# Opening of a two-layer hybrid encoder kernel: first input weights in four parts behind the modulation quarters, token factor applied to x early, one more slab and the offsets summed on TensorE, two low parts made on GpSimd

## The reference

```
c_act = silu(c)
mod   = c_act @ w_ada[0] + b_ada[0]        # (1, 3072): shift, scale, gate
h     = rms(x) * norm_w * (1 + scale) + shift
proj  = h @ w_in[0]                        # q, k, v are its first 768 columns
```

## Time and profile before

| | before |
|---|---|
| median of 3 runs | 1134.92 us |
| the profiled execution | 1134.01 us |
| its span, first to last instruction | 1132.3 us |
| TensorE busy | 1112.1 us, 98% of the span |
| DVE, ACT, POOL busy | 58%, 47%, 50% |
| mean granted TensorE clock | 0.994 |

### The profile page before, as it was taken

How to read it: one execution, slowest core, us unless ns; L and a number is a source line. 1 busy time by engine, 2 the same in 40 slices (tenths; PEclk the granted TensorE clock), 3 DMA queues, 4 the chain that set the end, 5 groups by cost and what they waited for, 6 DMA issues and landing times.

```text
span 1132.3 us, 15212 instructions
## 1 busy us (share of the span) xinstructions
PE 1112.1 (98%) x5807; PEld 917.6 (81%) x5807; DVE 660.6 (58%) x830; ACT 532.6 (47%) x930; POOL 561.7 (50%) x412
## 2 busy tenths in 40 slices
PE   6999999999999999999999999999999999999997
PEld 5778888888888888888898788888788887888885
DVE  4716465668788545538870635664887854131365
ACT  5544266655545533224462535666546553232234
POOL 5535444535445546545914363445355535464455
PEclk8999999999999999999999999999999999999999
DMA  9656423234443456653304463224433523443332
GB/s 322 208 134 197 132 76 93 76 112 131 129 119 84 129 177 199 206 156 104 96 20 101 142 205 93 76 75 120 130 99 99 132 73 87 116 133 94 105 100 93
DMA packets 203481, 140.79 MB, mean 124 GB/s; under 512 B 12001, under 2 KB 191249, under 8 KB 203409
## 3 DMA queue, kind: packets, MB, share of 16 engines
q1 hardware_dynamic: 202632, 138.91, 42.5%
q10 hardware_dynamic: 776, 0.91, 0.3%
HBM read 136.64 MB, written 2.63 MB: 123 GB/s over the span
## 4 chain that ended last, share of the span: by engine, by line
PE 95%; DVE 2%; SPq 1%; DMA 1%; issue 0%; POOL 0%; ACT 0%; DVEq 0%; POOLq 0%
PE main L683 77%; PE psC L683 6%; PE psA L683 5%; PE psB L683 4%; SPq L398 1%; DMA big<-in_w_ada 1%; PE psB L916 1%; PE psB L896 1%; DVE h_lo L1552 1%; SPq L426 0%; DVE psC L1505 0%; DVE tmp L1547 0%; PE psC L925 0%; POOL tmp L627 0%; DVE tmp L1505 0%
## 5 line engine op out<-in xcount | busy, mean ns | idle before, releaser
L601 POOL TENSOR_TENSOR w_lo<-raw,w_hi 128x512 fp32r<-128x512 f32 x344 | 502.3, 1481 | 537.4 <-ACT w_hi L1101 537.2
L683 PE MATMUL main<-h_hi,w_hi 128*128 128x512 f32 x976 | 388.7, 399 | 3.1 <-ACT h_hi L1101 2.9
L683 PE MATMUL main<-h_hi,w_lo 128*128 128x512 f32 x976 | 379.5, 390 | 0.0
L683 PE MATMUL main<-h_lo,w_hi 128*128 128x512 f32 x976 | 379.3, 390 | 0.0
L1101 ACT ACTIVATE w_hi<-raw 128x512 fp32r<-128x512 f32 x344 | 199.9, 623 | 286.1 <-PE main L683 161.8
L683 PEld LDWEIGHTS main<-h_hi,w_hi 128*128 128x128 f32 x976 | 183.6, 188 | 49.4 <-issue 11.1
L683 PEld LDWEIGHTS main<-h_hi,w_lo 128*128 128x128 f32 x976 | 183.2, 188 | 38.9
L683 PEld LDWEIGHTS main<-h_lo,w_hi 128*128 128x128 f32 x976 | 183.3, 188 | 38.0 <-issue 1.9
L1874 DVE TENSOR_TENSOR tmp<-main,misc 128x512 f32<-128x512 f32 x32 | 22.1, 692 | 165.3 <-PE main L683 162.8
L1713 DVE SCALAR_TENSOR_TENSOR misc<-main,cols,misc 128x511 f32<-128x511 f32 (+2 forms) x96 | 71.9, 749 | 60.9 <-ACT misc L1101 58.3
L683 PE MATMUL main<-y_hi,w_hi 128*128 128x512 f32 x256 | 100.5, 393 | 0.0
(11 more groups left out here) (288 smaller groups left out, 1411.8 us busy)
## 6 DMA issues: line engine op xcount, KB each, us to landing
raw<-in_w_in SPq DMA_DIRECT2D x124, 512.0 KB, 3.9
xbc<-in_w_ada SPq DMA_DIRECT2D x16, 512.0 KB, 4.9
zs<-in_w_ada SPq DMA_DIRECT2D x16, 512.0 KB, 4.6
raw<-in_w_pc SPq DMA_DIRECT2D x16, 512.0 KB, 3.8
raw<-in_w_out SPq DMA_DIRECT2D x16, 512.0 KB, 3.6
zs<-in_w_ada SPq DMA_DIRECT2D x16, 256.0 KB, 7.6
xbc<-in_w_in SPq DMA_DIRECT2D x8, 512.0 KB, 7.6
big<-in_w_ada SPq DMA_DIRECT2D x16, 256.0 KB, 7.2
```

The source lines that it names most:

```text
L601: nc.gpsimd.tensor_tensor(lo_b[:, cut, :], raw_b[:, cut, :], hi_b[:, cut, :].bitcast(F32), ALU.subtract).then_inc(s_split[b], 2 * BT_ // kt)
L683: return nc.tensor.matmul(o, a, b_, start=start, stop=stop)
```

## The change

1. **Weights in four parts.** `wide(part)` loads two k of all six tiles by two DMAs (256 KB and 512 KB, the latter with 512 columns in a row instead of 256) behind each quarter: q0, part 0, q1, part 1, q2, part 2, q3, part 3. ACT rounds a part by three instructions (two tiles each, `wide_hi_part`), POOL subtracts by three (`split_wide`). The number of elements of an instruction stays 512 a partition, and the number of instructions 12 in all.
2. **x takes the token factor early.** DVE multiplies xT by 1/rms in place (`x_scale`) for blocks 0 to 3: block 0 before the first modulation, 1 to 3 behind it. For these blocks ACT makes `h_hi` straight from xT with scale and shift (`h_high_first`), and no longer waits for h_32; DVE makes h_tmp with the shift in it from SBUF alone (`h_32_first`, a tensor_scalar). Blocks 4 to 7 keep the old way.
3. **TensorE sums one slab more** in quarter 0 (slab 4), behind the matmuls that spread 1/rms; DVE has five.
4. **TensorE adds the offsets** b_ada in each quarter by one matmul with the identity; `quarter_mod` has two small DVE operations instead of three.
5. **GpSimd makes the low parts of blocks 0 and 1**; DVE makes those of 2 to 7.
6. Orders: ACT does its quarter 2 products half before and half behind the high parts of blocks 2 and 3, and a part of the weights behind each quarter's products; POOL does part q of the weights, then the sums of quarter q+1.

```diff
-BY_PE = (2, 3)
+BY_PE = (2, 3, 4)
@@ SP
-            quarter(0)
-            wide(0)
-            quarter(1)
-            quarter(2)
-            wide(1)
-            quarter(3)
+            for q in range(QUARTERS):
+                quarter(q)
+                wide(q)
@@ POOL
+            def split_wide(part):
+                cut = slice(2 * part, 2 * part + 2)
+                for u in range(U_GA):
+                    pool.wait_ge(s_hiw, couple_count(u, 2 * part))
+                    nc.gpsimd.tensor_tensor(couple_lo[u][:, :, cut, :],
...
-                    for u, b in WIDE[:5]:
-                        split_half(l, u, b, 0)
-                    add_products(1)
-                    split_half(l, 2, 1, 0)
-                    add_products(2)
-                    for u, b in WIDE:
-                        split_half(l, u, b, 1)
-                    add_products(3)
+                    for q in range(QUARTERS):
+                        split_wide(q)
+                        if q < QUARTERS - 1:
+                            add_products(q + 1)
+                        if q == 0:
+                            for k in range(2):
+                                pool.wait_ge(s_h32, k + 1)
+                                pool.wait_ge(s_hhi, k + 1)
+                                nc.gpsimd.tensor_tensor(h_lo[:, k], h_tmp[k], h_hi[:, k].bitcast(F32), ALU.subtract
+                                                        ).then_inc(s_h, 1)
@@ PE, quarter_sums
+                pe.wait_ge(s_cols, 1)
+                mm(quarter_ps[q], ident[:, :],
+                   cols[:, 0, V_BADA:V_BADA + 2 * KT].rearrange("p (w k) -> p w k", w=2)[:, :, 2 * q:2 * q + 2], False, True
+                   ).then_inc(s_adam, 1)
...
             first_rows()
             spread(psC0, rms, 1)
+            slab_sums(BY_PE[2:])
             quarter_sums(0)
@@ ACT
+            def h_high_first(k):
+                act.wait_ge(s_mod, k // 2 + 1)
+                act.wait_ge(s_xs, k + 1)
+                f(h_hi[:, k, :], xT[:, k, :], ACT.Identity, scale=mod[:, 0, KT + k:KT + k + 1], bias=mod[:, 0, k:k + 1]
+                  ).then_inc(s_hhi, 1)
@@ DVE
             def quarter_mod(q):
+                k0, k1 = 2 * q, 2 * q + 2
                 dve.wait_ge(s_adam, q + 1)
-                modulation(0, quarter_ps[q], 2 * q, 2 * q + 2)
+                stt(mod[:, 0, KT + k0:KT + k1], quarter_ps[q][:, 2:4], 1.0, cols[:, 0, V_NORM + k0:V_NORM + k1], ALU.add,
+                    ALU.mult)
+                nc.vector.tensor_copy(mod[:, 0, k0:k1], quarter_ps[q][:, 0:2]).then_inc(s_mod, 1)
+                dve.wait_ge(s_mod, q + 1)
+            def x_scale(k):
+                tt(xT[:, k], xT[:, k], psC0, ALU.mult).then_inc(s_xs, 1)
+            def h_32_first(k):
+                dve.wait_ge(s_xs, k + 1)
+                ts_(h_tmp[k], xT[:, k], mod[:, 0, KT + k:KT + k + 1], mod[:, 0, k:k + 1], ALU.mult, ALU.add
+                    ).then_inc(s_h32, 1)
...
```

More of the change, by code:

```diff
@@ L209, in build @@
         s_raw, s_split = sem2("raw_loaded"), sem2("w_split")
-        s_rawx = [[sem(f"raw_wide_loaded{u}{half}") for half in range(2)] for u in range(3)]
+        s_xs, s_mod = sem("x_scaled_in_opening"), sem("modulation_done")
+        s_rawx = [sem(f"raw_wide_loaded{part}") for part in range(QUARTERS)]
         s_hi = sem2("w_hi_done")
@@ L408, in load @@
                 if (l, u) == (0, U_GA):
-                    for e in range(2):
-                        sp.wait_ge(s_split[e], part_count(0, 0, 1, e))
+                    sp.wait_ge(s_splitw, couple_count(0, KT - 1))
                 else:
@@ L842, in wide_pair @@
                 wide_low_rows(b)
-                for k in (a, b):
-                    wide_low_weights(k, range(len(tiles), len(WIDE)))
             def wide_end(i, k0):
@@ L1114, in w_hi_half, with wide_hi_part @@
                 f(hi_b[:, k:k + BT_, :], raw_b[:, k:k + BT_, :], ACT.Copy).then_inc(s_hi[b], 2 * BT_ // kt)
+            def wide_hi_part(part):
+                cut = slice(2 * part, 2 * part + 2)
+                for u in range(U_GA):
+                    act.wait_ge(s_rawx[part], 32)
+                    f(couple_hi[u][:, :, cut, :], couple_raw[u][:, cut, :].rearrange("p k (b n) -> p b k n", b=2), ACT.Copy
+                      ).then_inc(s_hiw, 1)
             def pre_hi(i):
@@ L1186, in h_high, with products @@
                 f(h_hi[:, k, tok], h_tmp[k % 4][:, tok], ACT.Identity, bias=mod[:, l, k:k + 1]).then_inc(s_hhi, 1)
-            def products(q):
-                for k in range(OWN[q]):
+            def products(q, ks=None):
+                for k in ks or range(OWN[q]):
                     act.wait_ge(s_ada[q % 2 * 4 + k // 2], (q // 2 + 1) * 32)
@@ L1592, in _ @@
                 if q == 0:
-                    dve.wait_ge(rms[3], 1)
-                    dve.wait_ge(s_xc, 2)
-                    dve.wait_ge(s_xca, 2)
-                h_32(0, 2 * q)
-                h_32(0, 2 * q + 1)
-                own = tuple((k - OWN[q + 1], k) for k in range(OWN[q + 1], KT)) if q < QUARTERS - 1 else ()
-                use_rows(q + 1, own[:-1] if q == 0 else own)
-                h_low(0, 2 * q)
-                h_low(0, 2 * q + 1)
-                if q == 0:
-                    use_rows(q + 1, own[-1:])
+                    x_scale(1)
+                for k in (2 * q, 2 * q + 1):
+                    if q < 2:
+                        h_32_first(k)
+                    else:
+                        h_32(0, k)
+                if q == 0:
+                    x_scale(2)
+                    x_scale(3)
+                if q < QUARTERS - 1:
+                    use_rows(q + 1, tuple((k - OWN[q + 1], k) for k in range(OWN[q + 1], KT)))
+                if q == 1:
+                    h_low_first(2)
+                    h_low_first(3)
+                elif q > 1:
+                    h_low(0, 2 * q)
+                    h_low(0, 2 * q + 1)
             dve.wait_ge(s_ds, 1)
```

101 lines of the change are left out of this document (54 added, 47 removed).

## The result

| | before | after |
|---|---|---|
| median | 1134.77 us (10 runs, 1134.13 to 1135.31) | 1137.51 us (10 runs, 1136.65 to 1139.59) |
| ratio | | 1.0026, 95% interval 1.0018 to 1.0034 |
| the profiled execution, its span | 1134.01, 1132.3 us | 1138.29, 1136.6 us |
| first matmul on h | 21.48 us | 22.82 us |
| first matmul of the last two blocks | 52.80 us | 56.76 us |

A forecast was written before the change was run, and what follows sets the result against it. TensorE is 98% busy, so only the opening can move, bound there by DVE's chain. 0.5 + 1.7 - 0.2 = +2.0 to 2.1 us makes 1134.01 into 1136.1, median 0.9 above: 1137.0; 8 in 10 from 1134.0 to 1139.1.

The forecast's parts named there:

- TensorE's own stream: TensorE's matmuls up to the last two blocks: could be there at 50.9 us at the earliest, so not the bound.
- Pair 4,5: DVE's two low parts of blocks 4 and 5, held by GpSimd's part 3: 3.1 us instead of 1.41, +1.7.
- Pair 2,3: DVE's two low parts of blocks 2 and 3, beside GpSimd's part 2: 3.1 us, middle of 2.5 to 3.6.
- TensorE waits 1.4 us and starts the sums of quarter 2 at 37.95: Before quarter 2's sums, TensorE waits for DVE's last slab, then starts at 37.95 us instead of 38.45.
- First matmul on h at 20.75: Opening: TensorE's first matmul on h comes at 20.75 us instead of 21.48, 0.7 us earlier.
- the clock rival: TensorE stays at 1.2 GHz for 7 to 8 more matmuls, or falls again at 36.5; 1138.6 us, chance 0.16.
- End at 54.9: End of the opening: first matmul of the last two blocks at 54.9 us instead of 52.80.
- The shorter modulation, -0.2: Modulation after the pair of blocks 4 and 5, with two links instead of three: -0.2 us.
- The slab on TensorE brings 0.2: Quarter 0: the slab handed from DVE to TensorE brings 0.2 us, not 0.86.
- h_32 from SBUF, 0.48 to 1.31 each: DVE's new h_32 form, first blocks: 0.48 us alone, up to 1.31 beside GpSimd, hidden.
- The clock falls in the new wait: TensorE's clock may fall again in the new 1.4 us wait at 36.5; each slow matmul costs 0.2 us.
- TensorE's own stream at 50.9 at the earliest, so it is not the bound: TensorE's matmuls would reach the last two blocks at 50.9 us at the earliest, ahead of DVE's chain at 54.9.

The follow-up runs named there:

- x6: Kernel before, with three more GpSimd subtractions into unread scratch right behind quarter 3's sums; 1136.04 us, 1.0011 of the kernel before.
- x2: Changed kernel, with GpSimd's parts 2 and 3 of the weights held until DVE's low parts up to blocks 3 and 5 are made; 1136.45 us.
- x9: Changed kernel with part 4 undone alone: DVE adds the offsets, without TensorE's identity matmul; 1137.86 us.
- x1: Changed kernel, with GpSimd's part 3 of the weights held until DVE's low parts up to block 5 are made; 1137.58 us.
- x3: x2 with TensorE's sums of quarter 2 moved behind both blocks' weight low parts; 1135.79 us, 1.0012 of the kernel before.
- x7: Changed kernel with slab 4 of quarter 0 back on DVE; 1137.75 us, 1.0028 of the kernel before.
- x11: The same kernel as x5, measured again beside the kernel before; 1134.23 us, 0.9996 of the kernel before.
- x5: x3, with the second and third instructions of part 3 also held until the low parts of blocks 6 and 7 are made; 1134.48 us.
- x10: x5 with part 4 undone too, so without TensorE's identity matmul for the offsets; 1133.86 us, 0.9995 of the kernel before.

## Why the prediction was right, point by point

The forecast was 1137.0 and the median is 1137.51. The mechanism is the one forecast, and one term beside it, TensorE's own stream, was wrong without harm to the number (last point).

- *Pair 4,5*: forecast 3.1 instead of 1.41, +1.7. Measured 3.24, +1.83; alone in x6, +1.84. Right, and it is the largest term.
- *Pair 2,3*: forecast 3.1, measured 3.19. Right. The size was luck in part: 3.1 was the middle of a range of 2.5 to 3.6, taken without a reason, for both pairs.
- *TensorE waits 1.4 us and starts the sums of quarter 2 at 37.95*: 1.25 us here, 1.26 in x2, 1.67 in x9 at 37.95. Right.
- *First matmul on h at 20.75*: 22.82 in the profile of the changed kernel and 22.56 in x1, but 20.72 to 21.21 in the nine other profiles whose start is the same or nearly so. The step is right for most and failed for the profiled execution: the forecast took the time from DVE's last slab and had TensorE's slab sums done by then. In the two late profiles the slab sums begin late (13.10 and 12.96) and the clock is at 0.50 from 14 us on. One of the two alone did little: x3 begins them at 13.03 with the clock at 1.00 and has 21.21, x9 begins at 12.44 with the clock at 0.53 in 14 to 16 and has 21.10. It is in part the clock rival, at another place than I had put it (I had named the matmuls behind 20 us and the new wait). It is also most of why the profiled time was missed by 2.2 us (1136.1 forecast, 1138.29) and the median by only 0.5: the profiled execution is the second slowest of the ten. When the other nine started is not known.
- *End at 54.9*: 56.76 here, less the 2.07 of the late start (if it passes through whole) 54.7; 54.77 in x7, 55.12 in x9. Right.
- *The shorter modulation, -0.2*: the traces show it. From the modulation of quarter 3 to h_32 it is 0.59 us before (49.86 to 50.45) and 0.25 after (54.07 to 54.32), -0.34. Of this x9, with three operations again, gives back 0.20 (0.45). In the medians it can't be told.
- *The slab on TensorE brings 0.2*: x7 is 0.4 slower than the changed kernel, and the first matmul on h of its profile, 21.11, lies among the 20.72 to 21.21 of the others. Nothing can be told at that size, as forecast.
- *h_32 from SBUF, 0.48 to 1.31 each*: two in 1.00 with POOL idle, two in 2.03 beside it. Right here, and hidden; beside POOL two took up to 2.92 (x11), more than 1.31 each.
- *The clock falls in the new wait*: it fell behind the wait in four of the five profiles that have it (0.50 in 42 to 44 here and in x1, in 40 to 42 in x2 and x7), and stayed at 1.00 in x9, whose wait is the longest (1.67). When it fell in the changed kernel it cost the end nothing: DVE's pair held the modulation of quarter 3 until 54.07, and TensorE had its sums done at 53.6.
- *TensorE's own stream at 50.9 at the earliest, so it is not the bound*: this was wrong, and nothing showed it as long as DVE was later. By the prediction's own numbers it is 37.95 + 1.05 + 54 x 0.23 + 1.05 = 52.5. And the clock adds to it: from the sums of quarter 2 to those of quarter 3 the changed kernel takes 12.39 us (40.00 to 52.39), the kernel before 10.42 (38.45 to 48.87); the offsets' matmul is 0.23 of the difference (40.91 to 41.14). The end in x2, where TensorE is the bound, is 54.63. So in the changed kernel DVE was later than TensorE by only 0.5 us.

From this last point follows what I had wrong afterwards, the reverse reading: that freeing one pair gives its 1.8 us back. Against the changed kernel x1 gave nothing, x2 0.7, x3 1.4, x5 2.7 us. DVE's two held pairs, a third (6,7) as soon as part 3 of the weights was moved beside it, and TensorE's wait with its slow matmuls hid one another, and only all together gave the loss back. How the 2.7 us divide among them is known for pair 4,5 alone, from x6 (1.4).

The Trainium skill says in "SBUF — State Buffer", section "Who interferes with whom", that a DVE instruction with two SBUF inputs contends with a GpSimd one that reads SBUF. x6 bears this out, with 3.25 us for two in place of 1.41. That section's words "fully blocks" for the whole instruction stand there for the 2-port modes. If they held here, each would wait up to POOL's 1.27 and last at most 2.0, an estimate; the held instructions of pairs 2,3 and 4,5 took 1.50 to 1.75 in the changed kernel, which agrees, since POOL's had been running for some 0.3 us when DVE's began (39.55 against 39.86, 50.63 against 50.91). The prediction put the tensor_scalar of h_32 under the same rule. It has one SBUF input of that size, and the section names tensor_scalar under the 2-port modes instead; held it was, two in 2.03 us against 1.00.

## What to carry to other kernels

- When work is moved on GpSimd, look at what stands beside it on DVE afterwards, in the timelines of both: in x6 three subtractions that GpSimd had time for cost 1.84 us on DVE's path, and no wait shows it, since a held instruction looks like a long one. Compare the length of the same form with and without a neighbour. In x5 the same form with one of its inputs in PSUM (h_32, 1.40 us for two at 40.06) was not held beside POOL's subtractions at 39.91 and 41.16.
- If such a hold is taken away and nothing comes back, look for what had become the bound, another hold or another engine, before giving up the theory; and check it from the other side, by putting the cost alone into the kernel that did not have it.
- Look behind the stage that was changed, too: in x5 and x10 most of what the opening gave was lost 50 us later in a wait for a weight that came hardly earlier.
- Moving a matmul or a slab between engines at the start brought less (0.4 to 0.6 us) than the slowest execution of a kernel differs from its fastest (2.9 us).

## What was not expected of the hardware

Beside a full POOL queue both of DVE's instructions of a pair are held. One line in the changed kernel (ns min/median/max of the two of pair 4,5), the same in x6, and x5's four, which had POOL idle:

```profile
L1594 DVE SCALAR_TENSOR_TENSOR h_lo<-tmp,mod,h_hi x2: 1568/1659/1750, 50.9 to 52.4; 128x512 fp32r<-128x512 f32 x2
```
```profile
L1555 DVE SCALAR_TENSOR_TENSOR h_lo<-tmp,mod,h_hi x2: 1554/1663/1772, 48.6 to 50.1; 128x512 fp32r<-128x512 f32 x2
```
```profile
L1596 DVE SCALAR_TENSOR_TENSOR h_lo<-tmp,mod,h_hi x4: 744/746/752, 47.9 to 51.8; 128x512 fp32r<-128x512 f32 x4
```

So a DVE instruction loses 0.8 to 1.0 us, and POOL's two beside it 0.4 us together (2.95 against 2.54): the loss is uneven, most of it DVE's. How much the first one loses depends on how much of POOL's instruction is left. Pair 2,3 of the kernel before began at 37.75, when POOL's subtraction of 36.78 (1.30 us) was nearly done: the first took 0.88 and only the second, which met a new one, 1.76:

```profile
L1552 DVE SCALAR_TENSOR_TENSOR h_lo<-tmp,mod,h_hi x2: 877/1317/1757, 37.8 to 38.5; 128x512 fp32r<-128x512 f32 x2
```

That fits the 2.56 of this pair there and its 3.19 in the changed kernel, where POOL's subtraction was 0.3 us old. Why the clock is at 1.2 GHz from 14 us on in some executions and from 16 us on in others stays open; no run here tells.
